# Attention inside a projection loop: every head's scores, transposes and value products one projection chunk later

## What is computed

```python
h = rmsnorm(x, norm_mix_g)
q, k, v, u_pool, gate_logits = split(h @ w_in)      # 512, 512, 512, 512, 2048 columns
q = apply_partial_rotary(rmsnorm(heads(q), q_norm_g), pos)   # 8 heads of 64
k = apply_partial_rotary(rmsnorm(heads(k), k_norm_g), pos)
attn = softmax(causal(q @ k.T) * 64 ** -0.5) @ heads(v)      # 256 tokens are one block
pooled = multiscale_pool_mixer(u_pool, w_pool, pool_scale)
gates = sigmoid(gate_logits + b_gate)               # two gates of 1024
mixed = gates[0] * (attn @ w_branch_attn) + gates[1] * (pooled @ w_branch_pool)
x = x + mixed @ w_out
```

## Time and profile before

| | |
|---|---|
| three runs, us | 1430.89, 1431.58, 1432.01 |
| span of the profiled execution, first to last instruction | 1429.2 |
| PE busy | 98% |
| DVE busy | 70% |
| ACT busy | 57% |
| POOL busy | 26% |
| the loop over `w_in` and the attention in it | up to 145.7 us of the span |

### The profile page before, as it was taken

How to read it: one execution, slowest core, us unless ns; L and a number is a source line. 1 busy time by engine, 2 the same in 40 slices (tenths; PEclk the granted TensorE clock), 3 DMA queues, 4 the chain that set the end, 5 groups by cost and what they waited for, 6 DMA issues and landing times.

```text
span 1429.2 us, 31475 instructions
## 1 busy us (share of the span) xinstructions
PE 1394.1 (98%) x11808; PEld 1299.6 (91%) x11808; DVE 1005.8 (70%) x1836; ACT 817.2 (57%) x1561; POOL 374.5 (26%) x194
## 2 busy tenths in 40 slices
PE   8989999999999998999999999999999999999998
PEld 8979889999979997999999999999998888888886
DVE  5488757878767687579964978888865555555554
ACT  6544646556556784355444567777764455554443
POOL 0260000000000293067884036767760000000001
PEclk9999999999999999999999999999999999999998
DMA  8447467767734301354555554444456656666661
GB/s 301 149 176 251 161 236 238 244 231 262 272 114 145 104 5 35 137 180 157 189 179 191 177 172 155 162 152 159 158 185 201 192 191 191 193 192 195 195 192 61
DMA packets 68948, 253.01 MB, mean 177 GB/s; under 512 B 7648, under 2 KB 7904, under 8 KB 68320
## 3 DMA queue, kind: packets, MB, share of 16 engines
q1 hardware_dynamic: 67680, 245.40, 51.7%
q10 hardware_dynamic: 1152, 5.98, 1.1%
HBM read 249.25 MB, written 2.10 MB: 176 GB/s over the span
## 4 chain that ended last, share of the span: by engine, by line
PE 87%; DVE 6%; ACT 3%; issue 3%; DMA 1%; POOL 0%; SPq 0%; DVEq 0%; ACTq 0%; POOLq 0%
PE bank L2287 24%; PE bank L1712 18%; PE bank L1713 18%; PE bank L1714 18%; PE bank L2251 1%; DVE w_lo L970 1%; ACT w_hi L512 1%; PE bank L2252 1%; PE bank L2097 1%; DVE arena L992 1%; DMA raw<-in_w_in 1%; PE bank L2235 0%; PE bank L1762 0%; ACT arena L790 0%; PE bank L1719 0%
## 5 line engine op out<-in xcount | busy, mean ns | idle before, releaser
L1712 PE MATMUL bank<-x_pair,w_hi 128*128 128x256 f32 x2120 | 613.5, 289 | 10.1 <-DVE x_pair L1014 3.4
L1713 PE MATMUL bank<-x_pair,w_hi 128*128 128x256 f32 x2120 | 599.8, 283 | 0.0
L1714 PE MATMUL bank<-x_pair,w_lo 128*128 128x256 f32 x2120 | 599.5, 283 | 0.0
L512 ACT ACTIVATE w_hi<-raw 128x1024 fp32r<-128x1024 f32 x416 | 438.1, 1053 | 191.3 <-PE bank L2287 167.7
L970 DVE TENSOR_TENSOR w_lo<-raw,w_hi 128x1024 fp32r<-128x1024 f32 x297 | 364.9, 1230 | 221.3 <-ACT w_hi L512 218.6
L1712 PEld LDWEIGHTS bank<-x_pair,w_hi 128*128 128x128 f32 x2120 | 406.2, 192 | 19.2 <-issue 5.1
L1713 PEld LDWEIGHTS bank<-x_pair,w_hi 128*128 128x128 f32 x2120 | 406.6, 192 | 0.2
L1714 PEld LDWEIGHTS bank<-x_pair,w_lo 128*128 128x128 f32 x2120 | 406.3, 192 | 0.0
L1641 POOL TENSOR_TENSOR w_lo<-raw,w_hi 128x1024 fp32r<-128x1024 f32 x119 | 285.9, 2403 | 223.9 <-ACT w_hi L512 149.9
L2287 PE MATMUL bank<-w_hi,x_pair 128*128 128x512 f32 x1016 | 272.0, 389 | 0.0
L2287 PEld LDWEIGHTS bank<-w_hi,x_pair 128*128 128x128 f32 x1016 | 190.7, 188 | 39.7
(11 more groups left out here) (344 smaller groups left out, 1528.4 us busy)
## 6 DMA issues: line engine op xcount, KB each, us to landing
raw<-in_u SPq DMA_DIRECT2D x128, 512.0 KB, 3.3
raw<-in_v SPq DMA_DIRECT2D x128, 512.0 KB, 4.3
raw<-in_w_in SPq DMA_DIRECT2D x54, 512.0 KB, 3.8
arena<-in_ada SPq DMA_DIRECT2D x48, 512.0 KB, 4.9
raw<-in_w_up SPq DMA_DIRECT2D x44, 512.0 KB, 4.7
raw<-in_w_down SPq DMA_DIRECT2D x22, 512.0 KB, 3.7
raw<-in_w_out SPq DMA_DIRECT2D x16, 512.0 KB, 4.1
raw<-in_w_q SPq DMA_DIRECT2D x16, 512.0 KB, 3.3
```

The lines of the kernel that those rows point to most:

```text
L512: act.activation(w_hi[:, s], raw[:, s], ACT.Copy).then_inc(hi_ready, 1)
L1712: pe.matmul(o, w, xh, start=start, stop=False, skip_group_check=True)
L1713: pe.matmul(o, w, xl, start=False, stop=False, skip_group_check=True)
L1714: return pe.matmul(o, wl, xh, start=False, stop=stop_, skip_group_check=True)
```

## The change

`score_at` and `turn_at` both give one more. So every score, turn and value product moves one chunk later in PE's queue, and `scores`, `exps`, `rows` and `turned` go one step later on DVE and ACT. The turn of the last head now falls on chunk 31, and its value product, which would be behind a chunk 32, is written out behind `pool_product(1)`. On ACT the last `turned` is no longer apart but in the loop's step 31. The eviction of block 1 waits for four heads instead of all eight; blocks 2 and 3 wait for eight as before.

```diff
 def score_at(h):
-    return 14 + h if h < 2 else 13 + 2 * h
+    return 15 + h if h < 2 else 14 + 2 * h
 
 
 def turn_at(h):
-    return 16 + 2 * h
+    return 17 + 2 * h
...
-                for h in range(HEADS - 1):
+                for h in range(HEADS):
                     if j == turn_at(h):
                         turned(h)
...
                 if j == 30:
                     pool_taken(0)
-                    turned(HEADS - 1)
             for f in range(1, 4):
-                act.wait_ge(S("head_out"), HEADS)
+                act.wait_ge(S("head_out"), 4 if f == 1 else HEADS)
...
                 if j == 31:
                     pool_product(1)
+                    attend(HEADS - 1)
```

## The result

| | before | changed |
|---|---|---|
| median of 16 runs each, us | 1430.87 | 1433.28 |
| lowest and highest | 1429.59 to 1432.05 | 1431.92 to 1436.76 |
| ratio changed / before, 95% interval | | 1.0019, 1.0012 to 1.0025 |
| profiled execution, us | | 1433.12 |
| its span, us | 1429.2 | 1431.3 |

The kernel became 2.4 us slower: just under the 0.2% (2.9 us) that the prediction named, above the forecast of 1432.0 and inside its range. A second set of 11 runs of the same text gave 1433.74 against 1430.41, ratio 1.0024 (1.0015 to 1.0033). So the loss is real, and larger than the 0.4 us that were forecast.

What follows compares the result with a forecast made beforehand. PE, busy 98% of the span, was taken to bound the kernel; only its waits could move. Terms -0.29 - 0.15 + 0 + 0.1 + 0.75 gave +0.4 us, on 1431.58 a forecast of 1432.0, range 1430.2 to 1434.2.

Steps and rivals of the forecast that it cites:

- (a): score(0) on PE comes behind a chunk instead of a rotation product: gain 0.29 us.
- (b): turn(0) and attend(0), 3.67 us late before: gain 0.15 us in case i, 1.2 in case ii.
- case i: POOL's L1655 starts before DVE's modulation_add(0) and holds the shared port pair: sum +0.4 us, chance 0.50.
- case ii: DVE's modulation_add(0) starts before POOL's L1655: sum 0.0, no change at 1431.6 us, chance 0.32.
- (c): turn(1) and attend(1), 1.73 us lost before: 1.7 taken, no difference, with bounds 0.4 and 2.3.
- (d): gates_scaled(0) moves between rows(2) and scores(3): loss 1.2 us instead of 1.06, 0.1 worse, or 0.7 in case ii.
- (e): Later heads: attend(5) loses 0.3 us, attend(6) 0.3, turn(7) 0.15, in all 0.75 worse.
- (f): End of the loop, turn(7) behind chunk 31 and attend(7) behind pool_product(1): loss 0 to 0.2 us, none in the sum.
- The slower rival: A POOL instruction gets in between L1066 and L1067 of rows(0), which ends past 83: 1434.8 us, chance 0.12.
- The faster rival: POOL is through before rows(1), so the head leaves the collisions: 1429.2 us, chance 0.06.

Runs made afterwards that it cites:

- the wait filled: Changed kernel with idle matmuls into an unused bank in head 0's two long waits, three ahead of turn(0) and four ahead of attend(0): 1431.70 us, ratio 1.0002.
- the filled kernels of either order: Idle matmuls laid into head 0's two long waits, in the changed kernel (1431.70 us, ratio 1.0002) and in the kernel before (1432.64 us, 1.0006).
- the last kernel: Changed kernel with scores ahead of the split, plus idle matmuls in waits at turn(0), turn(1) and the product with `w_out`: 1427.48 us, ratio 0.9971.

## Why the prediction was right or wrong

The mechanism was right and the sum too small: 0.4 us were forecast and 2.4 to 3.3 measured, of which the order of the loop makes 1.2 in three traces of it, and the clock, which the prediction did not speak of, 0.9 to 1.1 in the fit over the runs. Some 0.5 to 0.7 us of the pooled difference of 2.8 have no place of their own; at the 1.46 us that the fall near 177 cost, 1.25 stretches more would be 1.8 us and cover them, an estimate. The base was off too. The prediction put its sum of 0.4 on 1431.58, the median of three runs, 2.4 above the span; runs lie 1.7 to 1.9 above their spans, so the same sum gives 1431.4. That 1432.0 came nearer to 1433.28 was luck. By the steps of the prediction, each against its pace:

- **(a)** -0.29 forecast, -0.18 measured: score(1) starts 7.73 us behind the rotation product where the pace gives 7.62.
- **(b)** Forecast -0.15, or -1.2 by case ii; measured +0.42 (1.74 and 2.35, together 4.09, against 3.67). This is the step that failed. The question of case i or case ii, whether POOL's L1655 or DVE's L1080 starts first (L1654 and L1079 now), was decided by a third instruction. L1059 of before (L1058 now), the negative of the maxima, was costed as a small thing, and it was held for 2.37 us. L1079 then ran in 0.74, which the prediction would have read as case ii, but 1.8 us later than case ii had it start. Counted from the rotation product it ended 11.12 us behind, where case i had 11.26. So up to here the price was that of case i, though another instruction paid it. What the sum lacked came after it: POOL's L1656 took 2.45 instead of 2.12, and from the end of split 20 (83.83) to attend(0) it was 3.21 instead of 2.86. The second of these is L1058 again, now that of head 1: it took 0.61 beside POOL's L1659, 0.27 at its place in the kernel before. By the Trainium skill (SBUF — State Buffer, "Who interferes with whom"), a `tensor_scalar` can want the shared port pair beside DVE's own where a reduction can't, and the one that issues first holds the shared pair for its whole instruction. The trace agrees: L1058 was held and the two reductions just ahead of it weren't. The form, not the size, should have been priced.
- **(c)** No difference forecast; -0.34 measured, as 1.39 against 1.73. All of it lies in the half-clock chunk ahead of turn(1). With the wait filled, head 1 waits at attend(1) instead and reaches the same moment, so the term is right to 0.3, within its bounds.
- **(d)** +0.1 forecast, -0.09 measured (0.97 at attend(2) against 1.06). The places are as forecast: a wait at attend(2), none at turn(3) and attend(3). Moving `gates_scaled` put them back and left the sum.
- **(e)** +0.75 forecast, +1.2 measured, the other term that was sized too small: 0.57, 0.42 and 0.21 at attend(5), attend(6) and turn(7), for 0.3, 0.3 and 0.15. The places are right. At attend(5) I took the middle between two bounds, and it stood at the upper one, 0.6. Without the doubled addition attend(5) is on time, but the loss goes to the next head.
- **(f)** 0 forecast with a bound of 0.2; +0.31 measured. From turn(7) to the first `spread` it is 2.14, and the transposes, the pool product and the value product need 1.83. ACT's eviction of chunk 31 and its copy are the chain, as described. No run took this part alone, so the size stands, and its cause is argued.
- **The clock** had no term. The granted clock was 1.00 in every window of the attention in the trace before, and I took that one profile for the kernel. The second profile of the same text had a fall at 85.5 us.

These terms add up to +1.3, as 78.69 less 77.36 us has it (1.24 by the ends of ACT's instructions). The slower rival had the right sign and another mechanism: L1066 of rows(0) took 0.34, no instruction of POOL got in between, and rows(0) ended at 81.3, not past 83. The faster rival fell too, since POOL was busy up to 95.5 and head 1 ended its rows at 91.8. The marks that the prediction set for itself held (entries at attend(2), attend(6) and, of 0.12 us, turn(7), none at turn(3) and attend(3), no wait at a chunk, none at the spreads, 5.5 us in all). They left out the half-clock chunk, which the idle column doesn't show, and the 0.74 of L1079 pointed at case ii while the waits came out as in case i.

Open is why the changed kernel has more half-clock stretches on average. The fall near 177 to 180 us is in the profiles of both copies of the changed kernel and of five others (late heads alone, the addition moved in either way, the filled kernels of either order), and not in the other six (both profiles of before, the three with the scores first, `gates_scaled` moved), though but for the last kernel's filling PE's program there is the same in all. Two kernels with the change's tables and no filling are among those without it, and one with the tables of before is among those with it. PE stands twice for 1.1 us just ahead of that place in both kernels (1.08 and 1.14 before, 1.08 and 1.15 after), so the waits alone do not decide it. What does wasn't found.

## What to carry to other kernels

Where a latency chain (a head's scores, exponentials, transposes) shares a queue with bulk work, shifting the whole chain by one chunk only moves its waits: the terms (b) to (e) of this change were +0.4, -0.3, -0.1 and +1.2. What paid here is the order within the step, with the short piece that another engine waits for ahead of the bulk: under the new table it took the stage 4.1 us below the changed kernel and 2.8 below before, under the old table 1.7 below before, or 3.2 without a fall of the clock in that trace. And before a term under 2 us is believed, the granted clock of more than one profile of the same text should be read.

## What the runs showed of the hardware

- A tiny `tensor_scalar` of DVE, 128x2, was held 2.37 us beside a POOL instruction of 2.39, and to its end; the same form takes 0.17 behind 96 us, where POOL is through. The scale-and-mask from PSUM ahead of it (L1055, 0.55) and both reductions (0.29 and 0.41) took the same time beside POOL and without it.
- TensorE's granted clock went to 1.2 GHz for 3.4 us at a time, once for 6.8, in some runs of a text and not in others. Most of these falls stand behind waits of 1.1 to 2.3 us: with 1.12 and 2.33 us of standing next to head 0 the clock stayed at 1.00 in one profile of the kernel before and fell in the other. Four do not, and there PE had no wait above 0.55 us in the 13 us before: at 115.5 us in the last kernel, at 117.1 with `gates_scaled` moved, at 118.9 with only the late heads shifted, and at 607.8 in the changed kernel with the scores first. The first three came within the modulation sum or up to 1.4 us behind it, a stretch of 16 matmuls of one column each, which stands in all thirteen profiles and mostly without a fall:

```profile
112.19 1.95 PE L1764 MATMUL bank<-kept,arena 128*128 128x1 f32 x16
```

- Exposed, a fall cost 1.2 to 1.6 us in the stage and at the product with `w_out`; next to a wait that would have followed, nothing.
- The idle column does not show it. What shows it is the distance between PE's starts (0.21 us for 256 columns instead of 0.12) or the clock of an 8 us window.
